# The first block's queries and keys as merged 512-column matmuls in four banks each, and the first weight pieces over two DMA queues

## The reference, cut to what matters

```python
def first_block(x, norm_mix_pre, w_in, b_gate, pool_w, pool_scale, ...):
    u = rmsnorm(h, norm_mix_pre[l])
    z = u @ w_in[l]                        # 1024 -> 512 pool, 512 q, 512 k, 512 v, 2048 gates
    p = z[..., :o_q]
    q = z[..., o_q:o_k].reshape(B, S, N_HEADS, HEAD_DIM)
    k = z[..., o_k:o_v].reshape(B, S, N_HEADS, HEAD_DIM)
    v = z[..., o_v:o_g].reshape(B, S, N_HEADS, HEAD_DIM)
    g = z[..., o_g:] + b_gate[l]
    y_pool = pool_mixer(p, pool_w[l], pool_scale[l]) @ w_branch_pool[l]
    y_attn = moba_attention(q, k, v) @ w_branch_attn[l]
    m = jax.nn.sigmoid(g_pool) * y_pool + jax.nn.sigmoid(g_attn) * y_attn
    h = h + rmsnorm(m @ w_out[l], norm_mix_post[l])
    u2 = rmsnorm(h, norm_mlp_pre[l])
    a = jnp.square(jax.nn.relu(u2 @ w_up[l]))
    h = h + rmsnorm(a @ w_down[l], norm_mlp_post[l])
```

## Time and profile before

| | us |
|---|---|
| median of three runs | 1507.57 |
| the profiled execution, its own time | 1507.48 |
| its span | 1505.7 |
| TensorE busy | 1495.8 (99% of the span) |
| TensorE weight loads busy | 1288.3 (86%) |
| VectorE busy | 1020.7 (68%) |
| ScalarE busy | 785.1 (52%) |
| GpSimd busy | 54.7 (4%) |
| chain that ended last: TensorE, VectorE, ScalarE | 93%, 5%, 1% |

### The profile page before, as it was taken

One profiled execution on the slowest core, in us unless ns is written; L12 is line 12 of the kernel. 1 busy time (PEld: TensorE's weight loads), 2 busy tenths in 40 slices (PEclk: granted clock), 3 DMA queues, 4 the chain that ended last, 5 costly groups with the idle time before them and its releaser, 6 DMA issues.

```text
span 1505.7 us, 20960 instructions
## 1 busy us (share of the span) xinstructions
PE 1495.8 (99%) x8178; PEld 1288.3 (86%) x8178; DVE 1020.7 (68%) x1101; ACT 785.1 (52%) x899; POOL 54.7 (4%) x81
## 2 busy tenths in 40 slices
PE   9999999999999999999999999999999999999998
PEld 8878888888888888889888888888888888888886
DVE  5666766657566677987666667666567896676656
ACT  4554644446444465646544446444446655554444
POOL 0200100001000000010100001000000010000000
PEclk9999999999999999999999999999999999999999
DMA  9546455554555555353555455555545354355553
GB/s 375 201 146 246 168 190 184 184 195 168 195 191 175 213 197 175 141 195 112 196 190 189 179 195 196 199 191 195 191 172 200 137 195 168 112 196 195 188 191 124
DMA packets 40507, 280.44 MB, mean 186 GB/s; under 512 B 4608, under 2 KB 4864, under 8 KB 7040
## 3 DMA queue, kind: packets, MB, share of 16 engines
q1 hardware_dynamic: 39440, 275.08, 50.9%
q10 hardware_dynamic: 1008, 4.53, 0.8%
HBM read 277.49 MB, written 2.10 MB: 186 GB/s over the span
## 4 chain that ended last, share of the span: by engine, by line
PE 93%; DVE 5%; ACT 1%; issue 0%; DMA 0%; POOL 0%; SPq 0%; POOLq 0%; DVEq 0%; ACTq 0%
PE ps L399 90%; DVE w_lo L1514 2%; PE ps L624 1%; PE ps L616 1%; DVE accT L2014 0%; PE ps L666 0%; ACT Pb L1074 0%; DVE sT_lo L1521 0%; DMA raw<-stream_in 0%; DVE cu L2060 0%; DVE cu L2062 0%; ACT w_hi L1021 0%; DVE Pb L1547 0%; PE ps L970 0%; DVE Pb L1566 0%
## 5 line engine op out<-in xcount | busy, mean ns | idle before, releaser
L1514 DVE TENSOR_TENSOR w_lo<-raw,w_hi 128x2048 fp32r<-128x2048 f32 x250 | 571.5, 2290 | 256.0 <-ACT w_hi L1021 255.6
L1021 ACT ACTIVATE w_hi<-raw 128x2048 fp32r<-128x2048 f32 x251 | 479.8, 1914 | 291.2 <-PE ps L399 280.1
L399 PE MATMUL ps<-xT,w_hi 128*128 128x512 f32 (+1 forms) x2488 | 588.7, 378 | 0.0
L399 PEld LDWEIGHTS ps<-xT,w_hi 128*128 128x128 f32 x2488 | 444.5, 189 | 76.7 <-issue 0.2
L399 PE MATMUL ps<-xT,w_lo 128*128 128x256 f32 x2304 | 330.4, 282 | 0.0
L399 PEld LDWEIGHTS ps<-xT,w_lo 128*128 128x128 f32 x2304 | 314.9, 191 | 16.5
L399 PE MATMUL ps<-w_hi,sT_hi 128*128 128x512 f32 x576 | 186.2, 391 | 0.0
L399 PE MATMUL ps<-w_lo,sT_hi 128*128 128x512 f32 x576 | 185.5, 390 | 0.0
L399 PE MATMUL ps<-w_hi,sT_lo 128*128 128x512 f32 x576 | 185.3, 389 | 0.0
L399 PE MATMUL ps<-w_hi,xT 128*128 128x512 f32 x576 | 173.7, 392 | 1.3 <-ACT w_hi L1115 1.0
L399 PEld LDWEIGHTS ps<-w_hi,xT 128*128 128x128 f32 x576 | 107.7, 188 | 26.7 <-issue 3.2
(11 more groups left out here) (201 smaller groups left out, 932.0 us busy)
## 6 DMA issues: line engine op xcount, KB each, us to landing
raw<-stream_in SPq DMA_DIRECT2D x255, 1024.0 KB, 4.8
raw<-stream_in SPq DMA_DIRECT2D x4, 256.0 KB, 5.4
kTx<-mem_in SPq DMA_DIRECT2D x1, 1024.0 KB, 12.2
cu<-gate_bias_in SPq DMA_DIRECT2D x1, 1024.0 KB, 14.1
qk_tok<-post_gain_in ACTq DMA_DIRECT2D x1, 1024.0 KB, 5.2
kTx<-mem_in ACTq DMA_DIRECT2D x1, 1024.0 KB, 6.8
mem_kept<-kTx ACTq DMA_DIRECT2D x1, 1024.0 KB, 4.3
kTx<-mem_kept ACTq DMA_DIRECT2D x1, 1024.0 KB, 4.7
```

The lines of the kernel that those rows point to most:

```text
L399: return nc.tensor.matmul(bank_ap, lh, rh, start=start, stop=stop)
L1021: nc.scalar.activation(w_hi[:, slot(c), 0:width], raw[:, slot(c), 0:width], copy).then_inc(unit_hi, 1)
L1514: nc.vector.tensor_tensor(w_lo[:, slot(c), :], raw[:, slot(c), :], w_hi[:, slot(c), :].bitcast(F32), sub).then_inc(unit_lo, 1)
```

## The change

Queries and keys of the first block use `merged` in place of `flipped`. `merged` gets an argument `banks` for banks that don't lie side by side, and `rest_late`, with which it starts when the unit is rounded and waits for the remainder only ahead of the w_lo passes. q now lies in banks 2 to 5 and k in banks 0, 1, 6 and 7. The reciprocal row goes to bank 0, its turn behind the wait for `p`. Since banks 6 and 7 hold the pool means until `yT` has copied them out, the wait for `yT` stands ahead of unit 4 in TensorE's order. ScalarE copies the cross halves out (`q_cross`, `k_cross`, into two quarters of `Pb`), VectorE adds them (`q_sum`, `k_sum`) and scales the sum in place (`qT`, `kT`). The pool mixing waits for `q_sum`, unit 8 for `k_sum`, and the first scores for `kT`. Of unit 0's four pieces, numbers 0 and 2 are issued by ACT on its own queue, behind its two small transfers, and 1 and 3 by SP.

```diff
             for k in range(4):
                 cs = slice(k * 512, (k + 1) * 512)
-                sp.dma_start(raw[:, 0, cs], stream[0][:, cs]).then_inc(piece_landed[k] if k < 3 else unit_landed[0], 16)
+                if k % 2 == 1:
+                    sp.dma_start(raw[:, 0, cs], stream[0][:, cs]).then_inc(piece_landed[1] if k == 1 else unit_landed[0], 16)
...
-            def merged(r3, c, part, b, tiles=None, half_sem=None, fourth_free=None, free=(), between=None):
-                pe.wait_ge(unit_lo, upto_unit(r3, c))
+            def merged(r3, c, part, b, tiles=None, half_sem=None, fourth_free=None, free=(), between=None, banks=None, rest_late=False):
+                banks = banks or range(b, b + 4)
+                pe.wait_ge(unit_hi if rest_late else unit_lo, upto_unit(r3, c))
...
-                            mm(ps[:, b + f, :], wh[:, k, tile(f)], xT[:, kk, :, :].rearrange("p a n -> p (a n)"), kk == 0,
+                            mm(ps[:, banks[f], :], wh[:, k, tile(f)], xT[:, kk, :, :].rearrange("p a n -> p (a n)"), kk == 0,
                                False)
+                    if rest_late:
+                        pe.wait_ge(unit_lo, upto_unit(r3, c))
...
-            flipped(0, 2, 0, B, pieces=True)
-            inv_turn(ST_X)
+            merged(0, 2, 0, 2, rest_late=True)
             pe.wait_ge(b_act.sem, b_act.upto("p"))
+            inv_turn(ST_X, bank=0)
             pe.wait_ge(pool_in, 48)
...
-            flipped(0, 3, 1, B)
-
-            flipped(0, 4, 0, A)
+            merged(0, 3, 1, 2)
+
+            pe.wait_ge(inv_ready, 1)
             pe.wait_ge(b_dve.sem, BB("yT"))
+            merged(0, 4, 0, 0, banks=(0, 1, 6, 7))
+            pe.wait_ge(b_dve.sem, BB("q_sum"))
             for g in range(4):
                 last = mm(ps[:, 4 + g // 2, (g % 2) * S:(g % 2) * S + S], pw[:, g, :], yT[:, g, :], True, True)
             last.then_inc(b_pe.sem, b_pe.one("pool_mix"))
-            flipped(0, 5, 1, A)
-
-            pe.wait_ge(b_dve.sem, BB("qT"))
+            merged(0, 5, 1, 0, banks=(0, 1, 6, 7))
+
             wide(0, 6, 0, B)
...
                 if i == 0:
-                    pe.wait_ge(b_dve.sem, BB("kT"))
+                    pe.wait_ge(b_dve.sem, BB("k_sum"))
...
+                    if hp == 0:
+                        pe.wait_ge(b_dve.sem, BB("kT"))
                     scores(hp, False).then_inc(b_pe.sem, b_pe.one(f"S{hp}"))
...
             act.dma_start(colsA[:, 0:KT], cols[:, 0:KT]).then_inc(gain_in, 16)
+            for k in (0, 2):
+                cs = slice(k * 512, (k + 1) * 512)
+                act.dma_start(raw[:, 0, cs], stream[0][:, cs]).then_inc(piece_landed[k], 16)
...
             round_unit(0, 5)
+            used(0, 3)
+            nc.scalar.activation(tiles2(Pb[:, 1, :]), cross_of(2), copy)
+            did1(nc.scalar.activation(tiles2(Pb[:, 2, :]), cross_of(4), copy), "q_cross")
             round_unit(0, 6)
...
             round_unit(0, 7)
+            used(0, 5)
+            wait_dve1("q_sum")
+            nc.scalar.activation(tiles2(Pb[:, 1, :]), cross_of(0), copy)
+            did1(nc.scalar.activation(tiles2(Pb[:, 2, :]), cross_of(6), copy), "k_cross")
             round_unit(0, 8)
...
-            inv_copy(1)
+            inv_copy(1, bank=0)
             rest_unit(0, 4)
             rest_unit(0, 5)
             wait_pe1("pool_mean")
             did1(nc.vector.tensor_copy(yT, two_banks(6)), "yT")
-            used(0, 3)
-            did1(stt(out=qT, in0=two_banks(2), scalar=DH ** -0.5, in1=over(inv_row, 4), op0=mul, op1=mul), "qT")
+
+            def summed1(dst, banks):
+
+                for half in range(2):
+                    last = nc.vector.tensor_tensor(dst[:, 2 * half:2 * half + 2, :], main_of(banks[half]),
+                                                   tiles2(Pb[:, 1 + half, :]), add)
+                return last
+
+            wait_act1("q_cross")
+            did1(summed1(qT, (2, 4)), "q_sum")
+            wait_own1("q_sum")
+            did1(stt(out=qT, in0=qT, scalar=DH ** -0.5, in1=over(inv_row, 4), op0=mul, op1=mul), "qT")
...
-            used(0, 5)
-            did1(nc.vector.tensor_tensor(kT, two_banks(0), over(inv_row, 4), mul), "kT")
+            wait_act1("k_cross")
+            did1(summed1(kT, (0, 6)), "k_sum")
+            wait_own1("k_sum")
+            did1(nc.vector.tensor_tensor(kT, kT, over(inv_row, 4), mul), "kT")
```

More of the change, by code:

```diff
@@ L72 @@
          "PV2", "S3", "PT3", "PV3"]
-B1_ACT = ["p", "ypT_hi", "v", "exp0", "oT_hi0", "exp1", "oT_hi1", "exp2", "oT_hi2", "exp3",
+B1_ACT = ["p", "q_cross", "ypT_hi", "k_cross", "v", "exp0", "oT_hi0", "exp1", "oT_hi1", "exp2", "oT_hi2", "exp3",
           "sig0", "sig1", "sig2", "sig3", "oT_hi3"]
-B1_DVE = ["yT", "qT", "ypT_lo", "kT", "soft0", "rinv0", "pn0", "gate0", "PT0", "soft1", "rinv1", "pn1", "oT_lo0", "gate1", "PT1",
+B1_DVE = ["yT", "q_sum", "qT", "ypT_lo", "k_sum", "kT", "soft0", "rinv0", "pn0", "gate0", "PT0", "soft1", "rinv1", "pn1", "oT_lo0", "gate1", "PT1",
           "soft2", "rinv2", "pn2", "oT_lo1", "gate2", "PT2", "soft3", "rinv3", "pn3", "oT_lo2", "gate3", "PT3", "oT_lo3",
@@ L574, in some @@
                         for f in fs:
-                            last = mm(ps[:, b + f, 0:S], wl[:, k, tile(f)], xT_hi[:, kk, :], False, kk == KT - 1)
+                            last = mm(ps[:, banks[f], 0:S], wl[:, k, tile(f)], xT_hi[:, kk, :], False, kk == KT - 1)
                     return last
@@ L582, in merged @@
                             for f in range(4):
-                                mm(ps[:, b + f, 0:S], wh[:, k, tile(f)], xT_hi[:, k, :], k == 0, False)
-                                mm(ps[:, b + f, 0:S], wl[:, k, tile(f)], xT_hi[:, k, :], False, False)
+                                mm(ps[:, banks[f], 0:S], wh[:, k, tile(f)], xT_hi[:, k, :], k == 0, False)
+                                mm(ps[:, banks[f], 0:S], wl[:, k, tile(f)], xT_hi[:, k, :], False, False)
                         pe.wait_ge(turn_lo, tiles + 1)
@@ L587, in merged @@
                             for f in range(4):
-                                mm(ps[:, b + f, S:2 * S], wh[:, k, tile(f)], xT_lo[:, k, :], False, False)
+                                mm(ps[:, banks[f], S:2 * S], wh[:, k, tile(f)], xT_lo[:, k, :], False, False)
                         pe.wait_ge(turn_lo, tiles + 2)
```

## The result

| | before | after |
|---|---|---|
| median | 1507.58 us (6 runs, 1507.44 to 1507.79) | 1513.46 us (6 runs, 1512.87 to 1514.14) |
| ratio | | 1.0039, 95% interval 1.0029 to 1.0049 |
| profiled execution, its span | 1507.48, 1505.7 us | 1514.12, 1512.3 us |

The direction was right, the size was not: 1511.0 us was forecast with a range of 1510.0 to 1512.9, and the median lies 0.6 us above the range. The profiled execution is among the slower of its six runs; three lie at 1512.9 to 1513.0 and three at 1513.9 to 1514.1.

The account below looks back on a forecast made before the run. TensorE's stream was taken to bound the first 100 us. The wait's 4.1, less 0.38 for matmuls and 0.3 for the queue, gave 3.4 us later: 1510.9 profiled, 1511.0 us median, range 1510.0 to 1512.9.

Parts of the forecast that it names:

- Part 1, the matmuls: Merged q and k units on TensorE take 5.57 us instead of 5.76, saving 0.19 us each, 0.76 us for four.
- the 5.7 that the prediction named as a sign of being wrong: A merged unit on TensorE taking 5.7 us or more would show the forecast wrong; 5.6 us would show it right.
- Part 2, the wait for the copy: TensorE waits ahead of unit 4 for VectorE's `yT` copy, ending at 36.89 us; unit 4 starts 4.1 us late.
- Part 3, crosses and sums: ScalarE's four added copies and VectorE's four additions fall in idle time or slack and cost TensorE nothing; bounds 0 and 2.3 us.
- Part 4, two queues: First-piece shifts of at most 1.0 us are absorbed by TensorE's wait; unit 5 lands 0 to 1.3 us earlier, 0.3 taken.
- the forecast's bound of 1.0 us: At the start, the first weight piece gains at most 1.0 us or lands up to 1.0 us later.
- I take 0.3 us: Fuller transfers from 4 to 8 us make unit 5 land earlier and so advance `yT`: 0.3 us taken.
- the clock's fall: Rival: TensorE's clock halves in the 4.2 to 4.5 us gap before unit 4; +1.5 us, 1512.5 us, chance 0.25.
- Half of 3 us is lost: +1.5: Price of work at 1.2 GHz after the gap, taken from the warm-up phase at the start, some 3 us long.
- -0.38: Merged-form saving of units 4 and 5, behind TensorE's wait, the only part of the matmul saving that counts: 0.38 us.

Follow-up runs that it names:

- e4: The changed kernel with VectorE's pool-means copy ahead of the remainders of units 4 and 5, and unit 0's four pieces on SyncE's queue: 1506.92 us.
- e8: The kernel before with only TensorE's wait for the pool-means copy moved ahead of unit 4: 1513.76 us, ratio 1.0043.
- e2: The changed kernel with VectorE's pool-means copy ahead of the remainders of units 4 and 5, still two queues: 1507.54 us, ratio 1.0000.
- e5: The kernel before with only the queues changed, pieces 0 and 2 of unit 0 from ScalarE's queue: 1508.34 us, ratio 1.0006.
- e3: The changed kernel with all four pieces of unit 0 on SyncE's queue: 1513.17 us, ratio 1.0037.
- e7: The changed kernel with four warm-up calls (1.7 us) at the start of TensorE's wait for the pool-means copy: 1511.71 us, ratio 1.0028.
- e1: The changed kernel with eight warm-up calls (3.4 us) put into TensorE's wait for the pool-means copy: 1511.51 us, ratio 1.0027.

## Why the prediction was right or wrong

**Part 1, the matmuls: right.** The prediction worked out 0.76 us for four units. Measured are 0.71 between the best version (e4) and the kernel before, and 0.26 (of 0.38) for the queries alone. The 13 ns per start saved came from the rows, and a saving of 2.5 ns each would have given 0.16 us in all. The single units agree less evenly. Units 2 and 4 take 5.54 and 5.57 us in e4's trace, against 5.57 worked out. Units 3 and 5 take 5.69 and 5.77, the last above the 5.7 that the prediction named as a sign of being wrong. It isn't one: these two follow the pool matmuls, and in the kernel before they took 5.84 and 5.93 where the others took 5.76. The saving is 0.15 to 0.22 us in each.

**Part 2, the wait for the copy: right in place and cause, 4.26 us for 4.1.** The copy follows unit 5's remainder directly, TensorE waits once, and the one moved wait in the kernel before (e8) brings a loss of the full size. The idle stretch was 3.66 us, not 4.2 to 4.5, since the start came late.

**Part 3, crosses and sums: right that they cost nothing.** ScalarE's copies start at 33.53 and 34.02 us, VectorE's sums at 36.96, its scaling ends at 39.51 and unit 6's remainder starts at 39.87; TensorE's table has no wait for any of them.

**Part 4, two queues: the bounds right, the term wrong.** Within the forecast's bound of 1.0 us, the first piece lands 0.95 us later (7.41 for 6.46), and in the changed kernel the wait takes that in, as said. (Without the wait the medians show 0.62 and 0.71 us of it, e2 against e4 and e5.) But "I take 0.3 us" for unit 5's earlier landing failed: it was rounded at 31.67 us against 31.51, 0.16 later. The transfers moved 360 GB/s from 6 to 8 us instead of 306, and 251 instead of 260 from 4 to 6. That is about 0.09 MB more by 8 us, and still unit 5 didn't land earlier:

```profile
4.00:6.00 2.00, 2.00 (x12) 1.71 (x11) 0.05 (x1) 0.11 (x1) 0.00 (x0) 1.00 0.94 251
6.00:8.00 2.00, 0.91 (x5) 0.46 (x3) 1.70 (x4) 0.57 (x2) 0.00 (x0) 1.00 1.00 360
```

By the rule of the Trainium skill (DMA: Bandwidth & Descriptors, "Rules for kernel authors") this term is 0, which was nearer to what unit 5's landing shows, 0.16 us the other way, than the 0.3 taken.

**The step that failed: the clock's fall, left out of the sum with a chance of 0.25 and priced at "Half of 3 us is lost: +1.5".** It was a rival, and it is what happened, in every trace with the idle stretch unfilled (the changed kernel, e3 and e8). The price came from the warm-up at the start, about 3 us at half pace, as if the low stretch began when work resumes and always lasted that long. (The profile's granted clock reads 1.00 in that stretch of the start, so the phase was read from the pace alone. In nine of the other eleven traces it lasts longer and reaches into x's transposes, as eight that take up to 1.92 us instead of 1.04.) Measured, the loss was 2.77 us in the changed kernel and 1.70 in the one with one queue. The chance rested on a single fall, 3.7 us after the last matmul, held against a gap of 4.2 to 4.5; the fall came 2.5 us into the gap here and, in e7, at the end of one of 2.1 us.

With 4.26, -0.38 and 2.77 the sum would have been 6.65 for the profiled execution, as measured. In medians the forecast is 2.46 us too low: 1.95 is what filling the gap returns (e1), and the other 0.51 is in the main the 0.3 us that was taken for the queue and did not come and the 0.16 by which unit 5 was late.

Left open: what decides, from run to run, when the clock falls and when it comes back. It was low from 36.0 to 42.9 us in the changed kernel's trace, from 37.4 to 40.8 in e3, 36.9 to 40.4 in e7 and 37.2 to 40.6 in e8. The changed kernel's two groups of runs, 1.1 us apart, fit the two prices of 2.8 and 1.7 us, but only one of the six was traced.

## What to carry to other kernels

When new work takes a buffer whose last reader is a copy on another engine, look at what stands ahead of that copy in its engine's queue: here two remainders paced by transfers, which cost nothing until then. Moving the copy ahead of them gave the 5.9 us back, and with one queue as well the change gains 0.7. A gap of a few microseconds on TensorE has a second price, that of the clock after it, which came to 1.7 to 2.8 us on top of a unit that starts 4.3 us late; and a second DMA queue at the start brought forward nothing that was needed first in any of the seven kernels that had one.

## What the runs showed of the hardware

The granted clock fell after 2.5 us without matmuls in the changed kernel, and stayed at 1.2 GHz for 5.7 us of full work after it; in e3, e7 and e8 it fell within about 0.1 us of the moment at which work resumed and was back between 40.4 and 40.8 us. Warm-up matmuls in the gap kept it at 2.4 GHz in e1.

Two queues at the start made the first piece late: with 256 KB pieces on both queues it landed between 7.0 and 7.6 us in the traces of seven kernels, whichever queue it stood in, against 6.3 to 6.7 in the five with a single queue.
